# The last stage of a two-layer trunk: the multiplication by the gate is put on GpSimd, and the root of the norm one tile behind it

## The reference

```python
def rmsnorm(x, g):
    y = x32 * lax.rsqrt(jnp.mean(x32 * x32, axis=-1, keepdims=True) + EPS)
    return (y * g.astype(jnp.float32)).astype(x.dtype)
...
        y = y + gates[:, ex:ex + 1] * swiglu(xf, w_gu[ex], w_dn[ex])   # two non-zero gates for each token
...
    x = x + g2[:, None] * f
...
y_prompt = rmsnorm(x_ctx, final_norm_g)
y_sample = rmsnorm(x_lat, final_norm_g)
```

## Time and profile before

| what | value |
|---|---|
| time, median of 3 runs | 2905.55 us (2903.38 to 2905.74) |
| the profiled execution's own time | 2905.15 us |
| its span, first to last instruction | 2903.3 us |
| last stage, from the first gather's issue to the end of the span | 2862.9 to 2903.3 us |
| VectorE busy from 2874.0 to 2900.3 us | 24.82 us, 20 instructions |
| ScalarE busy in the same stretch | 10.01 us, 14 instructions |
| GpSimd busy in the same stretch | 11.82 us, 11 instructions |

### The profile page before, as it was taken

How to read it: one execution, slowest core, us unless ns; L and a number is a source line. 1 busy time by engine, 2 the same in 40 slices (tenths; PEclk the granted TensorE clock), 3 DMA queues, 4 the chain that set the end, 5 groups by cost and what they waited for, 6 DMA issues and landing times. The chain is left out here.

```text
span 2903.3 us, 46643 instructions
## 1 busy us (share of the span) xinstructions
PE 2647.4 (91%) x16147; PEld 2308.7 (80%) x16147; DVE 1672.7 (58%) x2418; ACT 1479.9 (51%) x2317; POOL 379.1 (13%) x522
## 2 busy tenths in 40 slices
PE   6997969999997999998979988886999999999993
PEld 5886958787884888887867778875999999999993
DVE  3345565555547423222241148854888888889896
ACT  3224655555543233331122246631888787878783
POOL 1222121111101400000130033304000000000002
PEclk9997979999998999999989989997999999999997
DMA  7531000000005322213316500033999999999995
GB/s 259 177 126 19 1 6 2 1 1 1 1 2 198 132 65 72 75 48 109 104 56 215 181 26 18 12 112 104 355 387 380 387 380 385 381 379 379 382 380 202
DMA packets 263225, 472.02 MB, mean 163 GB/s; under 512 B 29452, under 2 KB 202636, under 8 KB 256948
## 3 DMA queue, kind: packets, MB, share of 16 engines
q1 hardware_dynamic: 255600, 445.82, 43.6%
q0 software_dynamic: 4416, 14.70, 1.3%
q10 hardware_dynamic: 3076, 9.71, 0.9%
HBM read 453.67 MB, written 16.48 MB: 162 GB/s over the span
## 5 line engine op out<-in xcount | busy, mean ns | idle before, releaser
L3257 DVE TENSOR_TENSOR m_lo<-m_raw,m_hi 128x1408 fp32r<-128x1408 f32 (+1 forms) x459 | 648.9, 1458 | 62.6 <-ACT m_hi L3116 62.3
L3116 ACT ACTIVATE m_hi<-m_raw 128x1408 fp32r<-128x1408 f32 (+1 forms) x459 | 549.1, 1246 | 41.3 <-DMA m_raw<-moe_w_gu 23.2
L213 PE MATMUL acc<-w_hi,h_hi 128*128 128x512 f32 (+1 forms) x1120 | 431.9, 386 | 17.4 <-PEq L2676 7.8
L195 DVE TENSOR_TENSOR w_lo<-w_raw,w_hi 128x1024 fp32r<-128x1024 f32 (+1 forms) x132 | 160.8, 1221 | 495.5 <-ACT w_hi L190 494.8
L215 PE MATMUL acc<-w_hi,h_lo 128*128 128x512 f32 (+1 forms) x1120 | 425.3, 380 | 0.0
L214 PE MATMUL acc<-w_lo,h_hi 128*128 128x512 f32 (+1 forms) x1120 | 425.0, 380 | 0.0
L190 ACT ACTIVATE w_hi<-w_raw 128x1024 fp32r<-128x1024 f32 (+1 forms) x134 | 135.0, 1014 | 458.9 <-PE acc L215 400.9
L213 PEld LDWEIGHTS acc<-w_hi,h_hi 128*128 128x128 f32 x1120 | 213.2, 190 | 78.3 <-issue 33.3
L215 PEld LDWEIGHTS acc<-w_hi,h_lo 128*128 128x128 f32 x1120 | 213.0, 190 | 34.3
L214 PEld LDWEIGHTS acc<-w_lo,h_hi 128*128 128x128 f32 x1120 | 213.3, 190 | 32.5
L3034 PE MATMUL p_gates<-m_hi,x_hi 128*128 128x352 f32 x544 | 181.8, 334 | 5.0 <-DVE m_lo L3257 5.0
(11 more groups left out here) (399 smaller groups left out, 5333.5 us busy)
## 6 DMA issues: line engine op xcount, KB each, us to landing
m_raw<-moe_w_gu SPq DMA_DIRECT2D x544, 352.0 KB
m_raw<-moe_w_dn SPq DMA_DIRECT2D x187, 512.0 KB
ada_w<-ada_w SPq DMA_DIRECT2D x40, 1024.0 KB, 4.9
w_raw<-ffn_w_gu SPq DMA_DIRECT2D x88, 256.0 KB, 2.9
w_raw<-w_in_o SPq DMA_DIRECT2D x24, 512.0 KB, 5.7
w_raw<-ffn_w_dn SPq DMA_DIRECT2D x22, 512.0 KB, 3.5
w_raw<-w_in_e SPq DMA_DIRECT2D x28, 384.0 KB, 5.0
scratch_y_slots<-y_slot ACTq DMA_DIRECT2D x18, 512.0 KB, 6.4
```

Of the source, the lines that this page charges most:

```text
L195: eng.tensor_tensor(lo, self.raw_of(c, k), hi, ALU.subtract).then_inc(self.lo.sem, 1)
L213: eng.matmul(out, hi, whi[:, b, :], start=first, stop=False)
L3116: a.activation(whi[:, u % MSPLIT, 0:size(u)], raw[:, s, 0:size(u)], ACT.Copy).then_inc(s_hi.sem, 1)
L3257: dve.tensor_tensor(wlo[:, u % MSPLIT, 0:n], raw[:, u % MRAW, 0:n], whi[:, u % MSPLIT, 0:n], ALU.subtract).then_inc(s_lo.sem, 1)
```

## The change

GpSimd waits for the loads, and then multiplies by the gate for each tile as soon as VectorE has made the sum; mean and root of the tile before follow behind each multiplication, those of the last tile at the end. VectorE makes the sum one tile ahead: its order is sum(0), sum(1), add(0), sum(2), finish(0), add(1), sum(3), finish(1), add(2), sum(4), finish(2), add(3), finish(3), add(4), finish(4). Each add waits for GpSimd's multiplication of its tile. ScalarE's order stays; its square waits for the same add, which is now counted once per tile and not three times. Two semaphores are added, `s_summed` and `s_gated`.

```diff
-        s_weighted = K.sig("rt_exp")
+        s_weighted, s_summed, s_gated = K.sig("rt_exp"), K.sig("rt_logits"), K.sig("rt_rank")
...
-                for t in range(NT):
+                pool.wait_ge(loaded.sem, loaded.at(48))
+
+                def rstd(t):
                     pool.wait_ge(s_sq.sem, s_sq.at(t + 1))
                     pool.tensor_scalar(ss[:, 1, t:t + 1], ss[:, 0, t:t + 1], 1.0 / D, EPS, ALU.mult, ALU.add).then_inc(s_mean.sem, 1)
                     pool.wait_ge(s_mean.sem, s_mean.at(t + 1))
                     pool.tensor_tensor(ss[:, 2, t:t + 1], ss[:, 1, t:t + 1], K.minus_half[:], ALU.pow).then_inc(s_rstd.sem, 1)
 
+                for t in range(NT):
+                    y0 = picked[:, t, 0, :]
+                    pool.wait_ge(s_summed.sem, s_summed.at(t + 1))
+                    pool.tensor_tensor(y0, y0, gate[:, 1 if t else 0, :], ALU.mult).then_inc(s_gated.sem, 1)
+                    if t:
+                        rstd(t - 1)
+                rstd(NT - 1)
...
-                    a.wait_ge(s_v.sem, s_v.at(3 * (t + 1)))
+                    a.wait_ge(s_v.sem, s_v.at(t + 1))
...
-                def step(ins, n):
-                    ins.then_inc(s_v.sem, 1)
-                    dve.wait_ge(s_v.sem, s_v.at(n))
-
                 def finish(t):
                     dve.wait_ge(s_rstd.sem, s_rstd.at(t + 1))
                     dve.scalar_tensor_tensor(out[:, t, :], K.x[:, t, :], ss[:, 2, t:t + 1], g[:], ALU.mult, ALU.mult).then_inc(s_out.sem, 1)
 
-                dve.wait_ge(loaded.sem, loaded.at(48))
-                for t in range(NT):
+                def sum_rows(t):
+                    y0, y1 = picked[:, t, 0, :], picked[:, t, 1, :]
                     dve.wait_ge(gathered[t].sem, gathered[t].at(32))
                     dve.wait_ge(s_weighted.sem, s_weighted.at(t + 1))
-                    y0, y1, x = picked[:, t, 0, :], picked[:, t, 1, :], K.x[:, t, :]
-                    step(dve.scalar_tensor_tensor(y0, y1, K.weight[:, 1, t:t + 1], y0, ALU.mult, ALU.add), 3 * t + 1)
-                    step(dve.tensor_tensor(y0, y0, gate[:, 1 if t else 0, :], ALU.mult), 3 * t + 2)
-                    step(dve.tensor_tensor(x, x, y0, ALU.add), 3 * t + 3)
+                    dve.scalar_tensor_tensor(y0, y1, K.weight[:, 1, t:t + 1], y0, ALU.mult, ALU.add).then_inc(s_summed.sem, 1)
+
+                dve.wait_ge(loaded.sem, loaded.at(48))
+                sum_rows(0)
+                for t in range(NT):
+                    if t + 1 < NT:
+                        sum_rows(t + 1)
                     if t:
                         finish(t - 1)
+                    y0, x = picked[:, t, 0, :], K.x[:, t, :]
+                    dve.wait_ge(s_gated.sem, s_gated.at(t + 1))
+                    dve.tensor_tensor(x, x, y0, ALU.add).then_inc(s_v.sem, 1)
                 finish(NT - 1)
```

## The result

| | before | after |
|---|---|---|
| median, 5 runs each | 2905.74 us (2903.38 to 2913.8) | 2920.92 us (2920.06 to 2930.42) |
| profiled execution | 2905.15 us | 2920.5 us |
| its span | 2903.3 us | 2918.7 us |
| start of sum(0) to end of finish(4) | 26.14 us | 39.42 us |

The changed kernel is slower: the ratio is 1.0051, with a 95% interval of 1.0031 to 1.0072, that is 9 to 21 us. The forecast was 2918, in a range of 2912 to 2921, slower.

What follows compares the result with a forecast made beforehand. VectorE was taken to bound the stage at the kernel's end. Terms 2.18 + 4.91 + 3.04 + 3.05 - 0.48 gave 12.7 us on 2905.15, so 2918 us; range 2915 to 2920, or 2912 to 2921 with rivals and spread.

Steps and rivals of the forecast that it cites:

- sum(0) to the end of add(0): Start of the stage: sum(1) waits for gate(0), so the first addition ends later, +2.18 us.
- exclusion: VectorE instructions with two SBUF inputs and GpSimd's multiplication take turns, whole instruction by whole instruction; charged in full.
- Tile 1: Second tile: mean caught behind sum(2), gate(2) before finish(0); interval between additions 8.75 us, was 3.84, +4.91.
- Rival (b): Every tile goes as the second: mean caught behind sum(t+1); two more intervals of 8.75 us, 2919.2 us; chance 12%.
- Tiles 2 and 3: Middle tiles: finish(t-1), then the waiting gate(t+1), then add(t); intervals 8.08 us, +3.04 and +3.05.
- the loop: New closed chain add(t-1), square, weigh(t+1), sum(t+1), finish(t-1), add(t); 2.22 us from addition to weigh's end.
- Tile 4: Last tile, with no sum and no gate left before its addition: 4.55 us, was 5.03, -0.48.
- Tail: After the last addition: square, mean, root and finish(4) stay at 3.41 us.
- The list of signs: Timeline after: add(0) ending 5.9 to 6.0 us after sum(0) starts; sum(1), add(1) to add(3) at 2.2 to 3.5.
- Rival (a): No contention in this stage, only the closed chain through ScalarE: together +4.5 us, 2909.6 us; chance 7%.
- Rival (c): VectorE's relief counts, multiplication wholly beside VectorE, weighing off the closed chain: -2.3 us, 2902.8 us; chance 2%.
- Rival (d): GpSimd's multiplication costs 2.52 us or more: 1 to 2 us extra, 2919 to 2920 us; chance 7%.

Runs made afterwards that it cites:

- e1: Changed kernel with GpSimd multiplying only column 0 of each 128x1024 tile by the gate, waits and order kept; stage 30.71 us, one run 2907.45 us.
- e3: Changed kernel with VectorE's order sum(t+1), add(t), finish(t-1), so the add comes before finish; stage 30.84 us, one run 2901.28 us.
- e4: Changed kernel with the gate multiplication given back to VectorE, sum still one tile ahead; stage 37.02 us, one run 2919.61 us.
- e2: Changed kernel with ScalarE's weighing one more tile ahead, multiplication kept on GpSimd; stage 35.73 us, one run 2906.97 us.
- e7: Changed kernel with add(t) before finish(t-1) and ScalarE weighing two tiles ahead, all inputs in SBUF; stage 30.39 us, one run 2910.08 us.
- e6: Changed kernel with one PSUM input for sum and finish, add(t) before finish(t-1), weighing two tiles ahead; stage 24.86 us, median of 12 runs 2903.53 us.
- e5: Changed kernel, same order, weighed rows and final gain in PSUM, so sum and finish read one SBUF input; stage 34.24 us, one run 2919.44 us.

## Why the prediction was right, step by step

**sum(0) to the end of add(0).** Forecast 5.97 us (+2.18), measured 6.70. The mechanism was right (sum(1) ends 1.09 behind gate(0): 2881.70 behind 2880.61), but one thing was missed. I took GpSimd as free once the ten gathers were issued, and looked only at the multiplication for exclusion. But the issue of the last gather is held by VectorE's sum: where sum(0) starts first, it takes 1.81 us, and gate(0) can only follow. In e1, e3 and e4 it is caught as well (1.94, 1.77, 1.95), always where sum(0) was issued 0.14 to 0.32 earlier; in the trace before the gather came 0.03 earlier (0.93). e3's pair:

```profile
2865.49 1.28 DVE L3400 SCALAR_TENSOR_TENSOR picked_rows<-picked_rows,weight_of_choice 128x1024 f32<-128x1024 f32 x1 [20.55 <-ACT picked_rows L3378]
2865.81 1.77 POOL L3356 DMA_INDIRECT picked_rows<-scratch_y_slots,slot_of_choice  x1 [0.30 <-issue]
```

The other way round nothing is held. In e2 the gather's issue comes first, and the sum beside it takes its usual time:

```profile
2865.97 0.94 POOL L3356 DMA_INDIRECT picked_rows<-scratch_y_slots,slot_of_choice  x1 [0.30 <-issue]
2866.32 1.28 DVE L3401 SCALAR_TENSOR_TENSOR picked_rows<-picked_rows,weight_of_choice 128x1024 f32<-128x1024 f32 x1 [21.22 <-ACT picked_rows L3378]
```

In e2 and e7, where the last gather is issued first, the stretch is 6.00 us in both, the forecast's 5.97. So the term was mis-sized by 0.73 us, by a tie that the forecast didn't have.

**Tile 1.** Forecast 8.75, measured 8.58. I had the mean caught behind sum(2); it slipped in 0.02 us before it (2885.14 against 2885.16), and the root was caught in its place (1.48). The root so ended 4.05 us behind add(0) instead of 4.23, and that is the difference. The consequence, gate(2) before finish(0), was as forecast. Rival (b) wanted the same in tiles 2 and 3; it wasn't met there, by 0.23 us: root(1) ended at 2893.52, and sum(3) started at 2893.75.

**Tiles 2 and 3.** Forecast 8.08, measured 8.09 and 8.08: the loop's 2.33 us of idle time, sum and finish unhindered, the multiplication recorded at 3.32 and 3.31 us, the additions at 3.36. The sums started 0.07 later than forecast, and the multiplications ended 2.20 behind finish instead of 2.26; these two cancel. **Tile 4.** Forecast 4.55, measured 4.56. **Tail.** Forecast 3.41, measured 3.41.

**The list of signs** had sum(1) long (3.03) and the later additions long, which holds for add(2) and add(3); add(1) is 1.21 us, since finish(0) took the wait. That list contradicted my own sum there. Its first sign, add(0) ending 5.9 to 6.0 us after sum(0) starts, failed (6.70), for the gather.

**The rivals.** Rival (a), no contention, gave +4.5 us; e1, where the multiplication is too short to hold VectorE up, measured 4.57. Rival (c) wanted the weighing off the loop and the multiplication beside VectorE; it took e6 to build that. Rival (d) wanted a multiplication of 2.52 us or more; it took 2.35 from a free start. The split of the loss, a loop and an exclusion, is shown by e1, e2, e4 and e5. The two don't add up as separate prices: cutting the loop saves 3.69 us (e2), taking the length of the multiplication away 8.71 (e1), changing the order alone 8.58 (e3), since in e3's order the multiplication lies in the loop's idle time.

**The whole time, and the luck in it.** 13.28 us of the stage and 2.1 from before it make the 15.35 between the profiled executions. The part from before the stage was neither forecast nor caused by the change as far as the traces show: in e3 the same program reached sum(0) 10.7 us earlier. What moves the granted clock between executions wasn't studied. So what the forecast got right is the stage, 12.7 for 13.28, with +0.73 at its start and -0.17 in tile 1. That the median of the whole, 2920.92, still lies in the range, 0.08 us below its upper end, is luck: single executions of the kernel before, in 17 runs, lie up to 18 us apart, twice the width of the range.

## What to carry to other kernels

Before moving an instruction from one engine to another, write down the closed loop that its neighbours form: a step made one tile ahead brought nothing here, and cost 10.88 us (e4), while the step that feeds it was not made one tile further ahead as well. In this stage GpSimd's multiplication ran beside VectorE's instructions only where these had one operand in PSUM (1.28 us); with two in SBUF the pair took turns (3.03 to 3.37 us), and it paid to issue the instruction that others wait for before GpSimd could ask (8.58 us, e3). Where a stage is 1% of the kernel, measure it in the trace: there a difference of 0.5 us could be followed to single instructions, where 12 runs against 17 left 3 us open.

## What the hardware showed that I had not expected

- The issue of an indirect gather on GpSimd (0.93 to 0.94 us) is held up by a VectorE instruction with two SBUF inputs: 1.77 to 1.95 us in four traces, whenever VectorE's was issued first. It then ended 0.81 or 0.82 behind VectorE's, so that little more than 0.1 us of it was done before the wait. VectorE's instruction isn't held by it when the gather's issue comes first (1.28, 1.28 and 1.29 in the traces before, e2 and e7). The Trainium skill, SBUF — State Buffer, section "Who interferes with whom", infers that a tensor_tensor on VectorE, which with two SBUF inputs takes only a read interface from GpSimd, leaves descriptor generation alone; these rows, with a scalar_tensor_tensor of two SBUF inputs beside an indirect gather, say otherwise for that pair. Which part of the issue was held, the reading of the offsets or the writing of descriptors, no run tells.
- A GpSimd instruction on a 128x1 column, 0.19 us alone, costs what VectorE's instruction with two SBUF inputs has left to run, up to 1.3 us, when it comes second; in e6 that is what keeps the beat at 4.3 us. At 0.02 us the recorded starts don't tell which is second: in the changed kernel the mean recorded 0.02 before sum(2) took 0.19, in e6 those recorded 0.01 and 0.02 before add(2) and add(3) took 1.28. In e6 the addition stood right behind a running sum, in the changed kernel VectorE had been idle; whether that is the reason no run tells.
- The order of GpSimd and VectorE instructions that start 0.05 us apart decides whole microseconds: gate(2) issued 0.05 before finish(0) made a 1.28 us instruction one of 3.36.
